# Three accumulation passes per weight tile, each behind its own wait, and a later request for the LayerNorm sums

## The chip, the cores and the metric

The kernel runs on one core of one Trainium2 chip. The metric is device time in microseconds, as the median of three runs. Everything is float32 at the interface; on the chip every large product is made from pairs of reduced-precision parts.

## The reference, cut to what matters

One step of a two-layer streaming encoder, for 512 prompt tokens and 32 decode tokens (544 together), with D_MODEL = 2048:

```python
xp = layer_norm(x_prompt); xs = layer_norm(x_sample)
for l in range(2):
    z = x @ w_in[l]                 # heads of four attention groups, and a gate of 2048 columns
    mk, mv = split(mem_prompt @ w_mem_kv[l])          # 256 memory tokens
    outs = fox(...), band(...), sliding_window(...), cross(..., mk, mv)
    o = concat(outs) * silu(gate)
    x = layer_norm(ALPHA * x + o @ w_out[l])
```

The three products with `w_in`, `w_mem_kv` and `w_out` are nearly all of the work. The outputs are both streams after the second layer, and the keys, values and forget gates of each layer.

## The kernel before, in words

The activations stand transposed in the on-chip memory: 16 chunks of 128 features, each 544 tokens wide, worked on in two halves of 272 tokens. Weights come in tiles of 2048 x 128 (1 MB, `WR`). To keep float32 accuracy every operand is split into a high part and the rest: `WH` (a cast by ScalarE, `w_hi`, line 718) and `WL` = `WR` - `WH` (VectorE, `w_lo`, line 1034) for the weights, `XH` and `XL` for the tokens (`MTH` and `MTL` for the memory tokens). A product is WH*XH + WL*XH + WH*XL, accumulated in one bank of the accumulator memory. Each of the three names `WR`, `WH`, `WL` has two slots, so tile n+2 can be split only when TensorE has finished tile n: ScalarE waits for `zd`, casts and raises `hi`; VectorE waits for `hi`, subtracts and raises `lo`; TensorE waits for `lo`.

There are 184 weight tiles, 92 in each layer, in this order:

- 8 memory tiles (`mem_tile`, line 660), each 48 matmuls of 256 columns: 16 feature chunks k by three products. Between them stand transposes, a small product for the forget gates (`forget`, lines 610 and 617), and in layer 0 the transposes of the input tokens (`turn_x`, lines 639 and 645), which `TURNED` puts at given chunks of tiles 5 to 7.
- 52 head tiles (`gemm_half`, line 424), each two halves of 48 matmuls of 272 columns, with attention work between halves (`scores`, `turn_probs`, `mix`).
- 32 output tiles (`out_tile`, line 441), each 48 matmuls of 272 columns: first 16 tiles for the first half of the tokens (h = 0), then 16 for the second (h = 1). I number the output tiles of a half 0 to 15. Output tile 0 of a half is called with `split`: before each chunk it waits for that chunk of the gated attention output to be split (`ol[hf]`, VectorE's `o_lo`, line 1179; `oh[hf]` is ScalarE's `o_hi`, line 752).

In all three functions the loop over chunks is outside and the three products are inside, so WL is wanted by the second matmul of a tile.

LayerNorm is fused into the output tiles. VectorE adds the residual (line 1438, raises `zf`), subtracts a shift (`centre`, line 1240), adds to a running sum (line 1245), and later adds the squares that ScalarE made (lines 856 and 1250). The shift comes from a small TensorE product with a matrix of ones (`mean_of_first`, line 586, on output tile 0's result; ScalarE's `take_shift`, line 851, passes it on). At the end of a half, TensorE turns the running sums into statistics (`statistics`, line 596), ScalarE's `seed` (lines 862 to 865) and VectorE's `rstd` (lines 1258 to 1263) make the reciprocal deviation, and `normalise` applies it. These TensorE pieces are passed to a tile as `middle`, and run in front of chunk 8 of its 16: the mean in output tile 1 of each half, the sums of h = 0 in output tile 0 of h = 1, and the sums of h = 1 in memory tile 0 of layer 1 (in layer 1 they come after everything).

VectorE executes its instructions in the order written. For output tile c that order is: residual, centre, add up, `w_lo` of tile c+2, squares, `o_lo` or `normalise` or others. So `w_lo` of output tile 2 stands behind `centre` of output tile 0, and so behind the mean. In layer 0, half 0, tile 5 is followed by four subtractions for the next layer's memory tokens (`mem_lo`, line 1236). In layer 0's opening, VectorE's order is written out in `DVE_PLAN`: sums of the input rows, `w_lo` of tiles 2 to 4, the normalisation of the input rows (`first_norm`, line 1321), `w_lo` of tile 5, and then the sample rows (line 1331) and the affine steps, which follow TensorE's transposes.

Of the kernel before, what the change touches and what calls it, by code (L numbers as in the profile page):

```python
# [14 lines left out]
KC = DM // P  # L15
SEQ, DEC, PAST = 512, 32, 256
TOK = SEQ + DEC
HALF = TOK // 2
# [75 lines left out]
NQ = 4  # L94
# [47 lines left out]
def encoder_step(nc, wt, wff, bff, x_t, mem_t, fox_k, fox_v, fox_logf, band_k, band_v, swa_k, swa_v, mem_k, mem_v,  # L142
                 rel_pad, sinks, ln_gt, ln_bt, ident_d, causal_d, swa_mask_d, cos_d, sin_d,
                 y_o, fk_o, fv_o, fl_o, bk_o, bv_o, sk_o, sv_o, mk_o, mv_o):
    with ExitStack() as ctx:
# [6 lines left out]
        def sb(name, shape, dt=F32):  # L152
            size = 4
            for s in shape[1:]:
                size *= s
            off = top[0]
            top[0] += size + -size % 64
            return sb_at(name, shape, off, dt)

        def sem(name):  # L160
            return ctx.enter_context(nc.semaphore(name))

        GB = ctx.enter_context(nc.psum_tensor("GB", [P, 4, 512], F32))
        AB = ctx.enter_context(nc.psum_tensor("AB", [P, 4, 512], F32))

        XH = sb("XH", [P, KC, TOK], F32R)
        XT = sb_at("XT", [P, NT - 1, DM], top[0])
        XL = sb("XL", [P, KC, TOK], F32R)
        OY = sb("OY", [P, KC, TOK])
        WR = sb("WR", [P, 2, KC, P])  # L170
        WH = sb("WH", [P, 2, KC, P], F32R)
        WL = sb("WL", [P, 2, KC, P], F32R)
# [5 lines left out]
        MTH = sb("MTH", [P, KC, NMEM], F32R)  # L178
        MTR = sb_at("MTR", [P, KC, NMEM], top[0])
        MTL = sb("MTL", [P, KC, NMEM], F32R)  # L180
# [78 lines left out]
        hi = sem("hi")  # L259
        lo = sem("lo")  # L260
# [14 lines left out]
        m_hi = sem("m_hi")  # L275
        m_lo = sem("m_lo")
# [46 lines left out]
        oh = [sem("oh0"), sem("oh1")]  # L323
        ol = [sem("ol0"), sem("ol1")]
# [21 lines left out]
        def half(h):  # L346
            return slice(h * HALF, (h + 1) * HALF)
# [68 lines left out]
        def _(pe):  # L416
            def gemm_half(n, s, hf, free):

                if hf == 0:
                    pe.wait_ge(lo, n + 1)  # L420
                    pe.wait_ge(zf[s], free)
                for k in range(KC):
                    for i, (w, x) in enumerate(((WH, XH), (WL, XH), (WH, XL))):
                        mm = pe.matmul(GB[:, 2 * s + hf, 0:HALF], w[:, s, k, :],  # L424
                                       x[:, k, hf * HALF:(hf + 1) * HALF],
                                       start=(k == 0 and i == 0), stop=(k == KC - 1 and i == 2))
                if hf == 1:
                    mm.then_inc(zd, 1)
                return mm

            def out_tile(n, s, hf, free, split=None, middle=None):

                pe.wait_ge(lo, n + 1)
                pe.wait_ge(zf[s], free)
                for k in range(KC):
                    if split is not None:
                        pe.wait_ge(ol[hf], split * KC + k + 1)
                    if k == KC // 2 and middle is not None:
                        middle()
                    for i, (w, x) in enumerate(((WH, XH), (WL, XH), (WH, XL))):  # L440
                        mm = pe.matmul(GB[:, 2 * s + hf, 0:HALF], w[:, s, k, :], x[:, k, half(hf)],  # L441
                                       start=(k == 0 and i == 0), stop=(k == KC - 1 and i == 2))
                mm.then_inc(zd, 1)

            def gemm(n, m, j, hf=None):

                for h in (range(2) if hf is None else [hf]):
                    mm = gemm_half(n + j, j % 2, h, m + j // 2)
                return mm
# [183 lines left out]
            def turn_x(c):  # L633

                if c == 0:
                    pe.wait_ge(s_turn, 16 * N_TURN)
                    pe.wait_ge(x_norm, NT)
                    for k in range(KC):
                        mm = pe.transpose(AB[:, 3, DEC * k:DEC * (k + 1)], XTS[0:DEC, P * k:P * (k + 1)],
                                          ident[0:DEC, 0:DEC])  # L640
                    mm.then_inc(x_turn, 1)
                if c >= 3:
                    pe.wait_ge(nx, c - 2)
                for i in range(NT - 1):
                    mm = pe.transpose(AB[:, c % 3, P * i:P * (i + 1)], XT[:, i, P * c:P * (c + 1)], ident[:, :])
                mm.then_inc(x_turn, 1)

            def mem_tile(l, j, turned, middle=None):
                s, n = j % 2, l * LT + j
                pe.wait_ge(lo, n + 1)  # L650
                pe.wait_ge(zf[s], l * (LT // 2) + j // 2 + 1)
                for k in range(KC):
                    if j == 0 and k % (KC // NQ) == 0:
                        pe.wait_ge(m_lo, NQ * l + k // (KC // NQ) + 1)
                    if k in turned:
                        turn_x(turned[k])
                    if k == KC // 2 and middle is not None:
                        middle()
                    for i, (w, x) in enumerate(((WH, MTH), (WL, MTH), (WH, MTL))):
                        mm = pe.matmul(GB[:, 2 * s, 0:NMEM], w[:, s, k, :], x[:, k, :],  # L660
                                       start=(k == 0 and i == 0), stop=(k == KC - 1 and i == 2))
                mm.then_inc(zd, 1)

            pe.wait_ge(s_one, 1)
            for l in range(DEPTH):
# [7 lines left out]
                for kind, i in PE_PLAN[l]:  # L673
                    if kind == "mem":
                        mem_tile(l, i, TURNED.get(i, {}) if l == 0 else {}, last_sums if l and i == 0 else None)
                    elif kind == "forget":
                        forget(l, range(2) if l == 0 else [i], None if l and i == 0 else last_turn)
                    else:
                        turn_mem(l, i)
# [11 lines left out]
                for h in range(2):  # L691
                    n, m = l * LT + O0 + h * KC, l * (LT // 2) + (O0 + h * KC) // 2 + 1

                    def first_sums():
                        statistics(l + 1, [0])

                    def first_mean():
                        pe.wait_ge(zf[0], m + 1)
                        mean_of_first([half(h)], [h])

                    out_tile(n, 0, h, m, split=l, middle=first_sums if h == 1 else None)
                    out_tile(n + 1, 1, h, m, middle=first_mean)
                    with pe.Fori(1, KC // 2) as q:
                        nc.cur_bb.disable_value_cache()
                        for s in range(2):
                            out_tile(q * 2 + (n + s), s, h, q + m)
# [976 lines left out]
```

## Time and profile before

| | |
|---|---|
| median of 3 runs | 2032.47 us (2031.53 to 2033.11) |
| the profiled execution, its own time | 2032.19 us |
| its span, from the first to the last instruction | 2030.4 us |
| TensorE busy | 1982.9 us, 98% |
| VectorE busy | 1050.4 us, 52% |
| ScalarE busy | 704.8 us, 35% |
| GpSimd busy | 133.2 us, 7% |
| mean granted TensorE clock | 0.995 of full speed |

The profile was taken in one execution. 1.8 us of its time lie outside the span. Times in rows count from the start of the span. A row of the timeline has its start, its duration, the engine, the line, the operation, what it writes and reads, how many instructions are merged in it, and in brackets the idle time in front of it with what ended that. The duration of one matmul includes its latency, so it is longer than the distance to the next one; the rate is read from starts, or from a piece with its count.

### The profile page before, as it was taken

What the parts mean: (1) busy time and instruction counts of PE and PEld (TensorE: products, weight loads), DVE (VectorE), ACT (ScalarE), POOL (GpSimd) and SP (SyncE); (2) the same over time, 40 slices, a digit from 0 to 9 for tenths busy, and PEclk for the clock granted to TensorE, in tenths of its full rate; (3) what the DMA queues carried; (4) which work ended last, traced back from release to release, by engine and by line L of the source; (5) the groups of instructions that cost most, each with busy time, mean ns of one, the idle gap of its engine ahead of it and who ended that gap; (6) DMA issues with size and microseconds to landing.
All of it is one profiled execution on the core that took longest, in us unless ns stands there. A gap on an engine that the chain in (4) does not pass through costs nothing.

```text
span 2030.4 us, 38182 instructions
## 1 busy us (share of the span) xinstructions
PE 1982.9 (98%) x15868; PEld 1958.2 (96%) x15868; DVE 1050.4 (52%) x1649; ACT 704.8 (35%) x1053; POOL 133.2 (7%) x238
## 2 busy tenths in 40 slices
PE   6999999999999999999999999999999999999995
PEld 6999999999999999999999999999999999999995
DVE  6743343333465445777884334334335545566777
ACT  6432232222233233544563232222222322344444
POOL 0110000000000000000001001000000000000000
PEclk9999999999999999999999999999999999999998
DMA  7632232222222222555664223232222222225463
GB/s 303 222 139 96 105 106 80 104 96 92 93 72 97 71 88 90 194 193 185 225 210 150 89 105 107 78 105 85 92 104 89 79 75 82 102 90 193 185 213 136
DMA packets 55051, 254.75 MB, mean 125 GB/s; under 512 B 9469, under 2 KB 19325, under 8 KB 30865
## 3 DMA queue, kind: packets, MB, share of 16 engines
q1 hardware_dynamic: 31184, 202.68, 27.9%
q0 software_dynamic: 13344, 36.51, 5.2%
q10 hardware_dynamic: 10432, 14.29, 1.9%
q8 instruction: 65, 1.06, 0.2%
q14 instruction: 26, 0.21, 0.0%
HBM read 228.36 MB, written 27.70 MB: 126 GB/s over the span
## 4 chain that ended last, share of the span: by engine, by line
PE 94%; DVE 3%; DMA 1%; ACT 1%; issue 1%; SPq 0%; ACTq 0%; DVEq 0%
PE GB L424 62%; PE GB L441 18%; PE AB L470 3%; PE AB L513 3%; PE GB L660 3%; PE AB L481 2%; DMA WR<-in_wt 1%; DVE WL L1034 1%; PE AB L610 1%; ACT WH L718 1%; PE AB L518 0%; PE AB L498 0%; PE AB L521 0%; PE AB L617 0%; DVE OY L1275 0%
## 5 line engine op out<-in xcount | busy, mean ns | idle before, releaser
L424 PE MATMUL GB<-XH,WH 128*128 128x272 f32 x3328 | 965.0, 290 | 0.0
L424 PE MATMUL GB<-XL,WH 128*128 128x272 f32 x3328 | 958.4, 288 | 0.0
L424 PE MATMUL GB<-XH,WL 128*128 128x272 f32 x3328 | 957.9, 288 | 0.0
L424 PEld LDWEIGHTS GB<-XH,WH 128*128 128x128 f32 x3328 | 626.4, 188 | 1.5
L424 PEld LDWEIGHTS GB<-XH,WL 128*128 128x128 f32 x3328 | 626.4, 188 | 0.0
L424 PEld LDWEIGHTS GB<-XL,WH 128*128 128x128 f32 x3328 | 625.3, 188 | 0.0
L718 ACT CAST WH<-WR 128x2048 fp32r<-128x2048 f32 x184 | 351.2, 1909 | 746.6 <-PE GB L424 531.6
L1034 DVE TENSOR_TENSOR WL<-WR,WH 128x2048 fp32r<-128x2048 f32 x184 | 421.3, 2290 | 342.2 <-ACT WH L718 341.9
L441 PE MATMUL GB<-XH,WH 128*128 128x272 f32 x1024 | 296.2, 289 | 4.1 <-DVE WL L1034 4.1
L441 PE MATMUL GB<-XL,WH 128*128 128x272 f32 x1024 | 296.3, 289 | 0.0
L441 PE MATMUL GB<-XH,WL 128*128 128x272 f32 x1024 | 294.1, 287 | 0.0
L441 PEld LDWEIGHTS GB<-XH,WH 128*128 128x128 f32 x1024 | 192.6, 188 | 5.5 <-issue 5.2
L441 PEld LDWEIGHTS GB<-XH,WL 128*128 128x128 f32 x1024 | 192.9, 188 | 0.2
L441 PEld LDWEIGHTS GB<-XL,WH 128*128 128x128 f32 x1024 | 192.4, 188 | 0.0
L731 ACT ACTIVATE S<-S,nmx 128x256 f32<-128x256 f32 (+8 forms) x160 | 83.8, 524 | 175.3 <-DVE nmx L1076 173.6
L660 PE MATMUL GB<-MTH,WH 128*128 128x256 f32 x256 | 76.4, 298 | 19.1 <-DVE MTL L1236 11.7
L1141 DVE SCALAR_TENSOR_TENSOR SPL<-GB,SPL 128x544 fp32r<-128x544 f32 x24 | 17.3, 720 | 141.1 <-ACT SPL L777 141.1
L1107 DVE SCALAR_TENSOR_TENSOR GA<-ES,GB 128x544 f32<-128x544 f32 x30 | 21.5, 718 | 119.2 <-ACT ES L746 119.2
L1093 DVE COPY PT<-AB 128x512 f32<-128x512 f32 x64 | 40.1, 669 | 71.5 <-PE AB L481 71.5
L660 PE MATMUL GB<-MTL,WH 128*128 128x256 f32 x256 | 73.8, 288 | 0.0
L660 PE MATMUL GB<-MTH,WL 128*128 128x256 f32 x256 | 73.7, 288 | 0.0
L1076 DVE TENSOR_REDUCE nmx<-S 128x1 f32<-128x256 f32 (+8 forms) x160 | 69.8, 436 | 5.5
(178 smaller groups left out, 1640.9 us busy)
## 6 DMA issues: line engine op xcount, KB each, us to landing
WR<-in_wt SPq DMA_DIRECT2D x184, 1024.0 KB, 4.8
XR<-out POOLq DMA_DIRECT2D x64, 136.0 KB, 2.8
out<-OY ACTq DMA_DIRECT2D x24, 272.0 KB, 2.2
out<-OY ACTq DMA_DIRECT2D x8, 544.0 KB, 5.7
out<-KT POOLq DMA_DIRECT2D x16, 272.0 KB, 2.5
out<-VT POOLq DMA_DIRECT2D x16, 272.0 KB, 2.3
XT<-in_x_t SPq DMA_DIRECT2D x4, 1024.0 KB, 13.5
BI<-nc_rows POOLq DMA_DIRECT2D x8, 400.0 KB, 4.0
```

The lines of the kernel that those rows point to most:

```text
L424: mm = pe.matmul(GB[:, 2 * s + hf, 0:HALF], w[:, s, k, :], x[:, k, hf * HALF:(hf + 1) * HALF], start=(k == 0 and i == 0), stop=(k == KC - ...
L441: mm = pe.matmul(GB[:, 2 * s + hf, 0:HALF], w[:, s, k, :], x[:, k, half(hf)], start=(k == 0 and i == 0), stop=(k == KC - 1 and i == 2))
L470: mm = pe.matmul(AB[0:r, b, at:at + w], q[:, t0:t0 + r], k, start=(p == 0), stop=(p == 2))
L481: mm = pe.transpose(AB[:, j // 4, P * (j % 4):P * (j % 4 + 1)], S[:, at:at + P], ident[:, :])
L513: mm = pe.matmul(AB[:, 3, P * i:P * (i + 1)], V[:, kb, :], pt_col(j), start=(b == 0), stop=(b == len(g.blocks[i]) - 1))
L660: mm = pe.matmul(GB[:, 2 * s, 0:NMEM], w[:, s, k, :], x[:, k, :], start=(k == 0 and i == 0), stop=(k == KC - 1 and i == 2))
L718: act.copy(WH[:, s, :, :], WR[:, s, :, :]).then_inc(hi, 1)
L731: act.activation(s, s, ACT.Exp, bias=nmx[0:r, i:i + 1], accum_out=esum[0:r, i:i + 1]).then_inc(ex, 1)
L1034: dve.tensor_tensor(WL[:, s, :, :], WR[:, s, :, :], WH[:, s, :, :].bitcast(F32), ALU.subtract).then_inc(lo, 1)
L1076: dve.tensor_reduce(nmx[0:r, i:i + 1], S[0:r, at:at + w + g.sink], AX_X, ALU.max, negate=True).then_inc(mk, 1)
L1093: dve.tensor_copy(PT[:, 512 * b:512 * b + w], AB[:, b, 0:w]).then_inc(pte, 1)
L1107: dve.scalar_tensor_tensor(split2(GA[:, :]), split2(ES[:, :]), 1.0, z2(s), ALU.add, ALU.mult) \
```

## The change

In `gemm_half`, `out_tile` and `mem_tile` the nesting is turned round: the 48 matmuls of a half are now 16 of WH*XH, then 16 of WL*XH, then 16 of WH*XL. The tile begins behind `hi`, and `lo` is waited for only in front of the second pass. In a `split` tile the first pass waits for `oh` chunk by chunk and the third for `ol`; there chunk 15 is kept for the end of the tile in all three products. The same order of `out_tile` is used for all output tiles. `mem_tile` waits for the split memory tokens in the same way (`m_hi`, then `m_lo`). `middle` runs in front of matmul 40 of 48 in `out_tile`, where it ran in front of matmul 24; in `mem_tile` it stays at 24, and the transposes of `TURNED` stay at the same matmul numbers. Everything else is the same, and so are the number and the shapes of all instructions that compute.

```diff
             def gemm_half(n, s, hf, free):
                 if hf == 0:
-                    pe.wait_ge(lo, n + 1)
+                    pe.wait_ge(hi, n + 1)
                     pe.wait_ge(zf[s], free)
-                for k in range(KC):
-                    for i, (w, x) in enumerate(((WH, XH), (WL, XH), (WH, XL))):
+                for i, (w, x) in enumerate(((WH, XH), (WL, XH), (WH, XL))):
+                    if hf == 0 and i == 1:
+                        pe.wait_ge(lo, n + 1)
+                    for k in range(KC):
                         mm = pe.matmul(GB[:, 2 * s + hf, 0:HALF], w[:, s, k, :],
...
             def out_tile(n, s, hf, free, split=None, middle=None):
-                pe.wait_ge(lo, n + 1)
+                pe.wait_ge(hi, n + 1)
                 pe.wait_ge(zf[s], free)
-                for k in range(KC):
+                early = range(KC - 1)
+                order = [(i, k) for i in range(3) for k in early] + [(i, KC - 1) for i in range(3)]
+                for at, (i, k) in enumerate(order):
+                    w, x = ((WH, XH), (WL, XH), (WH, XL))[i]
+                    if at == KC - 1:
+                        pe.wait_ge(lo, n + 1)
                     if split is not None:
-                        pe.wait_ge(ol[hf], split * KC + k + 1)
-                    if k == KC // 2 and middle is not None:
+                        if i == 0:
+                            pe.wait_ge(oh[hf], split * KC + k + 1)
+                        if i == 2:
+                            pe.wait_ge(ol[hf], split * KC + k + 1)
+                    if at == 5 * KC // 2 and middle is not None:
                         middle()
...
             def mem_tile(l, j, turned, middle=None):
                 s, n = j % 2, l * LT + j
-                pe.wait_ge(lo, n + 1)
+                pe.wait_ge(hi, n + 1)
                 pe.wait_ge(zf[s], l * (LT // 2) + j // 2 + 1)
-                for k in range(KC):
-                    if j == 0 and k % (KC // NQ) == 0:
-                        pe.wait_ge(m_lo, NQ * l + k // (KC // NQ) + 1)
-                    if k in turned:
-                        turn_x(turned[k])
-                    if k == KC // 2 and middle is not None:
-                        middle()
-                    for i, (w, x) in enumerate(((WH, MTH), (WL, MTH), (WH, MTL))):
+                for i, (w, x) in enumerate(((WH, MTH), (WL, MTH), (WH, MTL))):
+                    if i == 1:
+                        pe.wait_ge(lo, n + 1)
+                    for k in range(KC):
+                        at = i * KC + k
+                        if j == 0 and k % (KC // NQ) == 0 and i != 1:
+                            pe.wait_ge(m_lo if i else m_hi, NQ * l + k // (KC // NQ) + 1)
+                        if at % 3 == 0 and at // 3 in turned:
+                            turn_x(turned[at // 3])
+                        if at == 3 * KC // 2 and middle is not None:
+                            middle()
```

## Rows read from the trace of the kernel before

**Rows 1.** The profile's page, busy time of each engine with its share and instructions.
```profile
PE 1982.9 (98%) x15868; PEld 1958.2 (96%) x15868; DVE 1050.4 (52%) x1649; ACT 704.8 (35%) x1053; POOL 133.2 (7%) x238
```
**Rows 2.** TensorE's waits: whom it waited for, us in total, times, longest.
```profile
PE GB L660 <- DVE MTL L1236: 11.7, 1, 11.7
PE GB L660 <- DVE WL L1034: 7.4, 5, 2.1
PE AB L596 <- DVE LNB L1250: 5.6, 3, 2.0
PE GB L441 <- DVE WL L1034: 4.1, 5, 1.0
```
**Rows 3.** Timeline of VectorE, the opening.
```profile
41.56 2.28 DVE L1034 TENSOR_TENSOR WL<-WR,WH 128x2048 fp32r<-128x2048 f32 x1
47.53 1.33 DVE L1321 TENSOR_SCALAR XTS<-XTS,XST 32x2048 f32<-32x2048 f32 x1
48.79 2.27 DVE L1034 TENSOR_TENSOR WL<-WR,WH 128x2048 fp32r<-128x2048 f32 x1
53.24 0.69 DVE L1331 TENSOR_TENSOR OY<-AB,gT 128x512 f32<-128x512 f32 x1 [2.18 <-PE AB L639]
```
**Rows 4.** Timeline of TensorE, the opening.
```profile
28.50 0.39 PE L660 MATMUL GB<-MTH,WH 128*128 128x256 f32 x1 [1.87 <-DVE WL L1034]
36.58 0.38 PE L660 MATMUL GB<-MTH,WH 128*128 128x256 f32 x1 [2.12 <-DVE WL L1034]
52.02 1.18 PE L639 MATMUL AB<-ident,XTS 32*128 32x32 f32 x16
```
**Rows 5.** Stretches of the opening: busy time by engine, clock, DMA share, GB/s.
```profile
29.00:34.00 5.00, 5.00 (x45) 5.00 (x44) 4.12 (x4) 2.06 (x3) 0.00 (x0) 1.00 1.04 397
36.50:40.00 3.50, 3.42 (x18) 3.42 (x19) 0.47 (x4) 3.23 (x7) 0.00 (x0) 0.61 0.61 204
```
**Rows 6.** Timeline around the first mean: TensorE and VectorE.
```profile
827.93 0.62 PE L586 MATMUL AB<-OY,ones 128*128 128x272 f32 x2
...
829.91 2.29 DVE L1034 TENSOR_TENSOR WL<-WR,WH 128x2048 fp32r<-128x2048 f32 x1
...
832.33 0.39 PE L441 MATMUL GB<-XH,WH 128*128 128x272 f32 x1 [0.77 <-DVE WL L1034]
832.56 0.29 PE L441 MATMUL GB<-XH,WL 128*128 128x272 f32 x1
832.68 0.28 PE L441 MATMUL GB<-XL,WH 128*128 128x272 f32 x1
```
**Rows 7.** Timeline at output tile 8 of the first half, TensorE.
```profile
868.62 0.29 PE L441 MATMUL GB<-XL,WH 128*128 128x272 f32 x1
869.95 0.39 PE L441 MATMUL GB<-XH,WH 128*128 128x272 f32 x1 [1.05 <-DVE WL L1034]
```
**Rows 8.** Timeline at the sums of the first half, layer 0, TensorE.
```profile
921.37 0.29 PE L441 MATMUL GB<-XL,WH 128*128 128x272 f32 x1
923.41 1.15 PE L596 MATMUL AB<-LNB,ones 128*128 128x272 f32 x4 [1.76 <-DVE LNB L1250]
```
**Rows 9.** Timeline at memory tile 2 of layer 1, TensorE.
```profile
1031.22 0.28 PE L660 MATMUL GB<-MTL,WH 128*128 128x256 f32 x1
1032.96 0.39 PE L660 MATMUL GB<-MTH,WH 128*128 128x256 f32 x1 [1.45 <-DVE WL L1034]
```
**Rows 10.** Pieces of the chain that ended last: start, us, what, matmuls.
```profile
89.48 30.13 PE GB L424 x240
819.05 9.04 PE GB L441 x72
869.95 48.70 PE GB L441 x384
934.81 84.40 PE GB L441 x672
1044.85 17.08 PE GB L660 x144
```

More of the change, by code:

```diff
@@ L431, in out_tile @@
             def out_tile(n, s, hf, free, split=None, middle=None):
-                pe.wait_ge(lo, n + 1)
+                pe.wait_ge(hi, n + 1)
                 pe.wait_ge(zf[s], free)
-                for k in range(KC):
-                    if split is not None:
-                        pe.wait_ge(ol[hf], split * KC + k + 1)
-                    if k == KC // 2 and middle is not None:
+                early = range(KC - 1)
[4 more added lines that the diff above has]
+                        pe.wait_ge(lo, n + 1)
+                    if split is not None:
+                        if i == 0:
[3 more added lines that the diff above has]
+                    if at == 5 * KC // 2 and middle is not None:
                         middle()
-                    for i, (w, x) in enumerate(((WH, XH), (WL, XH), (WH, XL))):
-                        mm = pe.matmul(GB[:, 2 * s + hf, 0:HALF], w[:, s, k, :], x[:, k, half(hf)],
-                                       start=(k == 0 and i == 0), stop=(k == KC - 1 and i == 2))
+                    mm = pe.matmul(GB[:, 2 * s + hf, 0:HALF], w[:, s, k, :], x[:, k, half(hf)],
+                                   start=(at == 0), stop=(at == 3 * KC - 1))
                 mm.then_inc(zd, 1)
@@ L649, in mem_tile @@
                 s, n = j % 2, l * LT + j
-                pe.wait_ge(lo, n + 1)
+                pe.wait_ge(hi, n + 1)
                 pe.wait_ge(zf[s], l * (LT // 2) + j // 2 + 1)
-                for k in range(KC):
-                    if j == 0 and k % (KC // NQ) == 0:
-                        pe.wait_ge(m_lo, NQ * l + k // (KC // NQ) + 1)
-                    if k in turned:
-                        turn_x(turned[k])
-                    if k == KC // 2 and middle is not None:
-                        middle()
-                    for i, (w, x) in enumerate(((WH, MTH), (WL, MTH), (WH, MTL))):
+                for i, (w, x) in enumerate(((WH, MTH), (WL, MTH), (WH, MTL))):
[9 more added lines that the diff above has]
+                            middle()
                         mm = pe.matmul(GB[:, 2 * s, 0:NMEM], w[:, s, k, :], x[:, k, :],
-                                       start=(k == 0 and i == 0), stop=(k == KC - 1 and i == 2))
+                                       start=(at == 0), stop=(at == 3 * KC - 1))
                 mm.then_inc(zd, 1)
```

## The prediction

> **What bounds the kernel now.** I read the page first: TensorE is busy 98% of the span and VectorE 52% [rows 1], so time can come only from TensorE's idle time or from the pace of its matmuls. The view of TensorE's waits then gives the idle time: 11.7 us before its first matmul, five waits for WL in the memory tiles, 7.4 us, three for the running sums, 5.6 us, and five for WL in the output tiles, 4.1 us [rows 2]. Nothing else holds it. I then went to the timeline at each wait, to see who is late and what that engine was held by. The pace comes from the chain: 240 head matmuls in 30.13 us, 672 of the output tiles in 84.40 us, 125.5 ns each; 144 memory matmuls in 17.08 us, 118.6 ns each [rows 10]. One pass of 16 is therefore 2.0 us (1.9 in a memory tile). That is what the change gives each tile: the deadline for `lo` moves 2.0 us back, and the tile begins behind `hi`, which is ready at least one VectorE subtraction (2.29 us, [rows 6]) earlier. A tile that now waits less than 2.0 us for WL loses its wait; one that waits longer, or whose WL moves back too, does not.
>
> **The opening (gain 3.0 us).** Here WL is not late because of TensorE but because of VectorE's and ScalarE's own queues, so gains of successive tiles do not add up: each tile ends at its `lo` plus two passes, where it ended at `lo` plus three. Memory tile 4: VectorE ends its WL at 41.56 + 2.28 = 43.84 [rows 3]. Two passes later (32 x 118.6 ns = 3.8) TensorE is at 47.6. Memory tile 5 now starts on its WH pass and comes after six matmuls (0.7 us) to the transposes of the input rows, at 48.4. These need the last normalised rows, which VectorE has at 47.53 + 1.33 = 48.86 [rows 3]. So they start at about 49.0, where they start at 52.02 [rows 4]: 3.0 us. WL of tile 5 (48.79 + 2.27 = 51.06 [rows 3]) is asked for ten matmuls and one more set of transposes later, past 52, and no longer holds anything. Next in line is VectorE: it waited 2.18 us for those transposes before the sample rows at 53.24 [rows 3], and can start them at 51.1, 2.1 us earlier; the remaining 0.9 us of TensorE's lead meet VectorE's short waits for later transposes, so I keep 3.0 and take 2.1 as the low end. The first matmul itself comes earlier too (it waits only for MTH, not MTL), but memory tiles 1 to 4 wait for weights that have their own pace, so nothing is added for it. The upper end is 4.0: tile 5's own pass and the transposes in it.
>
> The clock: an idle time of 1.87 us in front of 28.50 left it at 2.4 GHz (granted 1.00 in the stretch behind it), one of 2.12 us in front of 36.58 was followed by a stretch with 0.61, mostly at the 1.2 GHz level [rows 4, 5]. After the change idle times there are 2.0 us or less, so it may stay up. I count nothing for it: tile 4 then waits for its own WH anyway.
>
> **Output tiles, the mean (gain 0).** The wait of 0.77 us in output tile 2 stands 4.40 us behind the mean: 827.93 to 832.33 [rows 6]. Between them lie ScalarE's shift, `centre`, the sum and `w_lo`, all behind the mean. Now the mean runs 16 matmuls later and `lo` is wanted 16 matmuls later. Both move together: 24 matmuls lie between them before and after (8 + 16 in place of 24). Four such waits, two in each layer, make up 4 x 0.77 = 3.1 of the 4.1 us that the output tiles wait for WL [rows 2]; they stay, inside the tile between the WH*XH and the WL*XH pass. The two moves together cost nothing and bring nothing here.
>
> **Output tile 8, layer 0, first half (gain 1.3 us).** WL is late behind `mem_lo`, which hangs on tile 5. The distance of starts is 869.95 - 868.62 = 1.33 us for a normal 0.13, and the restart costs 0.1 (832.33 to 832.56 is 0.23 us, the next distance 0.12 [rows 6]). 1.33 < 2.0, so it all goes: 1.2 + 0.1 = 1.3 [rows 7]. Layer 1 has no such wait.
>
> **The sums (gain 1.9 us in each layer).** The sums start at 923.41, 2.04 us after the last matmul at 921.37 [rows 8]. They are held by VectorE's squares of the half before. Asked for 16 matmuls later (2.0 us), they start at the same moment, but the 16 matmuls are already done. 2.04 - 0.13 = 1.9; the three waits of the view include the layer 1 one, of the same length, and the last after all tiles, which the change does not touch. What follows (ScalarE's seed, `rstd`, then the residual and the mean) starts at the same moment as before and is wanted at the same moment, because the mean too has moved 16 matmuls back. So 3.8 for both.
>
> **Memory tile 2, layer 1 (gain 1.7 us).** WL stands behind `rstd`, which hangs on sums at matmul 24 of tile 0, unchanged. The distance of starts is 1.73 us [rows 9] for 0.12; with the restart 1.7, less than the 1.9 of a pass. What is late next is the split of the last tokens for the forget gates (line 617); VectorE makes it right behind, and TensorE asks for it after a whole tile, 5.7 us.
>
> **The waits themselves (0).** There are 184 new waits for `lo`, and in the four split tiles 16 more each. The piece of 240 head matmuls holds two tile borders with two met waits each and runs at 125.5 ns throughout; the piece of 72 from 819.05 holds output tile 0 with its 16 met waits for `ol` and takes 9.04 us, 125.6 ns each [rows 10]. So a met wait costs nothing that I can see; the other bound is a restart of 0.1 us each [rows 6]. I take 0, the value of the rows that show the thing itself. Queued behind the new wait is the rest of the tile, and behind that everything; ScalarE's next `w_hi` waits for the tile's end, as before.
>
> A rule of the Trainium skill speaks against this. Its page Perfetto Trace Analysis, section Identifying Dependency Chains, says that waits beyond an instruction's own can become separate instructions in front of it, and the page Advanced Engine Details and Errata, section Network/Comms, gives 50 to 100 ns for reading a semaphore from the sequencer; by that 184 waits would be an estimated 9 to 18 us. By that rule the time would be no better or worse than now. The trace does not show the price at any met wait, as said.
>
> **The order of the matmuls (0).** Their number, shapes and bank are the same. Which weight part is loaded while which token part streams is the same set of pairs, only k differs. But the pace is not one number: the 384 matmuls from 869.95 take 48.70 us; without the restart and the tail of the last one (some 0.3) that is 126.1 ns, where the 672 later ones have 125.2 to 125.6 [rows 10]. I can't tell what sets this. The bounds for the new order are 125.0 and 126.1, that is -0.5 and +0.6 ns on 13,056 matmuls of 272 columns (104 head tiles of 96, 64 output tiles of 48): -6.5 to +8 us. I take 0.
>
> **The sum.** 3.0 + 1.3 + 3.8 + 1.7 = 9.8 us. 2032.2 - 9.8 = 2022.4 for the profiled execution; the median of the runs is 0.3 above it: 2022.7.
>
> **The rivals.**
> - A, the pace moves. For it: 125.2 and 126.1 ns stand in the same loop. Against: the piece over three kinds of pairs is even. A slow pace gives 2022.7 + 8 = 2030.7, a fast one 2016.2.
> - B, slower than before: each new wait breaks the run of weight loads and costs a restart, 184 x 0.1 = 18.4 us, so 2041. It decides from 9.8/184 = 53 ns a wait; the time is then above 2032.5. For it: a wait that holds costs 0.1 us. Against it: the pieces with met waits.
> - C, given back: TensorE's lead in the opening and in layer 1's memory tiles is lost again to VectorE and to the transfers, as VectorE is little idle there. Only the sums and tile 8 stay: 3.8 + 1.3 = 5.1, so 2027.4.
> - D, the moved mean is not neutral: if the chain behind it reaches later tiles (output tile 3, or the residuals that free the bank), each of four places costs up to a pass of 2.0, 8 us, and leaves 2030.7.
>
> **Chances.** Forecast (2018.5 to 2026) 0.58; A slow 0.12, A fast 0.08; B 0.07; C 0.10; D 0.05. The range 2016 to 2030 takes in the forecast, C, and all of both A but the slow end, and leaves out B and D. A measurement of this kernel can tell 0.2%, 4 us, from no change. Faster by more than that, below 2028.4: the forecast, A fast, C and a third of A slow, 0.80. Within: the rest of A slow and D, 0.13. Slower: B, 0.07.
>
> **What would show it.** In TensorE's waits of the changed kernel: the sums wait once (2 us, at the end) instead of three times; four waits of about 0.8 us are left in the output tiles, now between WH*XH and WL*XH matmuls, none at tile 8; layer 1's memory tile 2 starts without idle time; the first matmul starts earlier than 11.7 and the transposes of the sample rows near 49. The step on the waits is wrong if borders between passes show more than 0.13 us. The step on the pace is wrong if 48 matmuls of an output tile take more than 6.07 or less than 5.98 us. The prediction is wrong if TensorE's busy pieces are longer by some 10 us in sum, or if new waits stand where there were none.

## The result and the profile after

The changed kernel takes 2021.13 us (median of 4, 2020.73 to 2021.17) where the one before takes 2032.79 (median of 4): a ratio of 0.9944, 95% interval 0.9931 to 0.9956. The forecast was 2022.7, with a range of 2016 to 2030. The profiled execution took 2021.17 us, its span 2019.4 us against 2030.4 before.

The page of the kernel after, span and busy times:

```profile
span 2019.4 us, 38302 instructions
PE 1981.5 (98%) x15868; PEld 1956.7 (97%) x15868; DVE 1049.7 (52%) x1649; ACT 705.0 (35%) x1053; POOL 133.4 (7%) x238
```

TensorE is busy for 1.4 us less than in [rows 1], and the span is 11.0 us shorter: what went is idle time and, it turns out, a little pace. The view of TensorE's waits, with its total, times and the longest, to set against [rows 2]. Lines have moved: L450 is `out_tile`, L672 `mem_tile`, L1046 `w_lo`, L605 the sums, L859 the cast of the memory tokens, L907 the copy of a memory tile out of its bank.

```profile
PE GB L672 <- ACT MTH L859: 8.9, 1, 8.9
PE GB L450 <- DVE WL L1046: 3.3, 4, 0.8
PE GB L672 <- ACT MT L907: 2.4, 2, 2.1
PE AB L605 <- DVE LNB L1262: 2.0, 1, 2.0
PE GB L672 <- DVE WL L1046: 1.6, 2, 1.4
PE GB L672 <- ACT WH L730: 0.6, 1, 0.6
PE AB L648 <- DVE XTS L1333: 0.3, 1, 0.3
```

The sums wait once instead of three times. Four waits for WL of 0.8 us are left in the output tiles, one fewer than before. In the memory tiles five waits for WL have become two, and waits for WH and for the bank have come up in their place.

The timeline of TensorE after, with rows left out at each `...`: the opening's transposes; the mean in output tile 1 (line 595) and the wait behind it in tile 2; the first pass of output tile 8; the sums and the matmuls behind them; and the start of layer 1's memory tile 2. At the edge of a stretch a row has only the matmuls inside the stretch.

```profile
48.98 1.15 PE L648 MATMUL AB<-ident,XTS 32*128 32x32 f32 x16 [0.34 <-DVE XTS L1333]
...
826.57 0.62 PE L595 MATMUL AB<-OY,ones 128*128 128x272 f32 x2
...
828.77 1.27 PE L450 MATMUL GB<-XH,WH 128*128 128x272 f32 x9
830.88 0.64 PE L450 MATMUL GB<-XH,WL 128*128 128x272 f32 x3 [0.84 <-DVE WL L1046]
...
865.12 1.17 PE L450 MATMUL GB<-XH,WH 128*128 128x272 f32 x8
...
918.17 1.08 PE L605 MATMUL AB<-LNB,ones 128*128 128x272 f32 x4
918.88 0.99 PE L450 MATMUL GB<-XL,WH 128*128 128x272 f32 x5
...
1024.50 0.76 PE L672 MATMUL GB<-MTH,WH 128*128 128x256 f32 x5
```

A row without brackets had no idle time in front of it that the view counts. The transposes start at 48.98 where [rows 4] has 52.02. Output tile 8, the sums and layer 1's memory tile 2 (1024.50) have lost the waits of [rows 7, 8, 9]. The wait behind the mean is still 0.84 us, where [rows 6] has 0.77, but it now stands between WH*XH and WL*XH.

How far TensorE's tiles are ahead of the kernel before gives the account. The lead is the difference of the starts of the same tile in the two timelines, taken before rounding, and the last column is how much it changed since the row above. The rows without a layer are layer 0's:

| up to the start of | before, us | after, us | lead | this step |
|---|---|---|---|---|
| layer 0, memory tile 6 | 60.93 | 57.85 | 3.07 | opening 3.07 |
| output tile 0 | 818.89 | 815.58 | 3.31 | 52 head tiles 0.24 |
| output tile 7 | 862.69 | 859.12 | 3.58 | 0.27 |
| output tile 8 | 869.95 | 865.12 | 4.84 | 1.26 |
| second half, tile 0 | 918.48 | 913.12 | 5.37 | 0.53 |
| second half, tile 1 | 927.40 | 920.08 | 7.32 | sums 1.96 |
| second half, tile 3 | 940.92 | 933.73 | 7.19 | -0.13 |
| layer 1, memory tile 1 | 1025.64 | 1018.80 | 6.84 | -0.35 |
| layer 1, memory tile 2 | 1032.96 | 1024.50 | 8.46 | 1.62 |
| layer 1, output tile 0 | 1809.55 | 1800.73 | 8.82 | 0.36 |
| layer 1, second half, tile 0 | 1907.83 | 1898.27 | 9.56 | 0.74 |
| layer 1, second half, tile 1 | 1916.75 | 1905.24 | 11.52 | sums 1.96 |
| end | 2030.39 | 2019.37 | 11.02 | -0.50 |

### The profile page after: what moved, and what is told of

Same layout as the page of the kernel before. It is cut to its first block, busy times and chain, and to the rows that moved or that the text cites. A ratio compares the mean times of both kernels' runs of the same rounds, so it can differ in the third digit from the quotient of the medians.

```text
span 2019.4 us, 38302 instructions
## 1 busy us (share of the span) xinstructions
PE 1981.5 (98%) x15868; PEld 1956.7 (97%) x15868; DVE 1049.7 (52%) x1649; ACT 705.0 (35%) x1053; POOL 133.4 (7%) x238
## 4 chain that ended last, share of the span: by engine, by line
PE 96%; DVE 2%; DMA 1%; ACT 1%; issue 0%; SPq 0%; ACTq 0%; DVEq 0%
PE GB L426 62%; PE GB L450 19%; PE AB L479 3%; PE AB L522 3%; PE GB L672 3%; PE AB L490 2%; DMA WR<-in_wt 1%; PE AB L619 1%; DVE WL L1046 1%; PE AB L527 0%; PE AB L507 0%; PE AB L530 0%; PE AB L626 0%; PE AB L654 0%; PE AB L494 0%; DVE OY L1287 0%
## 5 line engine op out<-in xcount | busy, mean ns | idle before, releaser
L1046 DVE TENSOR_TENSOR WL<-WR,WH 128x2048 fp32r<-128x2048 f32 x184 | 421.4, 2290 | 344.3 <-ACT WH L730 344.0
L426 PE MATMUL GB<-XH,WH 128*128 128x272 f32 x3328 | 458.1, 290 | 0.0
L426 PE MATMUL GB<-XL,WH 128*128 128x272 f32 x3328 | 451.3, 287 | 0.0
L426 PE MATMUL GB<-XH,WL 128*128 128x272 f32 x3328 | 451.2, 287 | 0.0
L426 PEld LDWEIGHTS GB<-XL,WH 128*128 128x128 f32 x3328 | 431.2, 189 | 0.0
L426 PEld LDWEIGHTS GB<-XH,WL 128*128 128x128 f32 x3328 | 431.2, 189 | 0.0
L426 PEld LDWEIGHTS GB<-XH,WH 128*128 128x128 f32 x3328 | 429.5, 188 | 1.5
L450 PE MATMUL GB<-XH,WL 128*128 128x272 f32 x1024 | 149.7, 288 | 3.3 <-DVE WL L1046 3.3
L450 PE MATMUL GB<-XL,WH 128*128 128x272 f32 x1024 | 151.3, 288 | 0.0
L450 PE MATMUL GB<-XH,WH 128*128 128x272 f32 x1024 | 149.2, 287 | 0.0
L450 PEld LDWEIGHTS GB<-XH,WL 128*128 128x128 f32 x1024 | 136.4, 188 | 4.2 <-DVE WL L1046 4.2
L450 PEld LDWEIGHTS GB<-XL,WH 128*128 128x128 f32 x1024 | 137.1, 188 | 0.5
L450 PEld LDWEIGHTS GB<-XH,WH 128*128 128x128 f32 x1024 | 136.3, 188 | 0.0
L479 PE MATMUL AB<-SPL 128*128 128x256 f32 (+6 forms) x552 | 70.3, 279 | 0.0
L479 PEld LDWEIGHTS AB<-SPL 128*128 128x128 f32 (+1 forms) x552 | 64.7, 164 | 4.1
L522 PE MATMUL AB<-PT,V 128*128 128x128 f32 x560 | 67.6, 275 | 0.0
```

The lines of the kernel that those rows point to most:

```text
L479: mm = pe.matmul(AB[0:r, b, at:at + w], q[:, t0:t0 + r], k, start=(p == 0), stop=(p == 2))
L522: mm = pe.matmul(AB[:, 3, P * i:P * (i + 1)], V[:, kb, :], pt_col(j), start=(b == 0), stop=(b == len(g.blocks[i]) - 1))
L1046: dve.tensor_tensor(WL[:, s, :, :], WR[:, s, :, :], WH[:, s, :, :].bitcast(F32), ALU.subtract).then_inc(lo, 1)
```

## The experiments

Each time stands against the kernel before, run beside it on the same chip; the edits shown are against the changed kernel, but for the second one, which is against the kernel before. Its median there was 2033.1 in the first group (passes alone, deeper alone, the first order alone, memory tiles as before), 2033.8 in the second, 2033.3 for the last run. The changed kernel's own runs were not repeated beside them, so a difference from 2021.1 is good to about a microsecond: the median of the kernel before moved by that much between the groups and the result above (2032.8 to 2033.8).

**The passes without the later mean and sums.**

```diff
-                    if at == 5 * KC // 2 and middle is not None:
+                    if at == 3 * KC // 2 and middle is not None:
```

> The changed kernel with the mean and the sums back in front of matmul 24 of their output tiles; the three passes and their waits stay. My theory: the two halves of the change touch different waits. With the mean at 24 and lo wanted at matmul 15 of output tile 2, 39 matmuls (4.9 us) lie between them against a chain of 4.4 us, so the four waits of 0.8 us behind the mean (in all 3.7 us with restarts) vanish, while the two waits for the sums of 1.9 us each come back: +3.8 - 3.7, so about 2021.2 us, as the changed kernel. In the trace: TensorE waits for LNB three times, for WL in the output tiles not at all. Rival: the later place of the mean is what the kernel gains by, and the mean's waits stay wherever it is; then both come back and the time is about 2025.

Measured: 2020.76 us, ratio 0.9941 (0.9927 to 0.9954). TensorE's waits:

```profile
PE AB L605 <- DVE LNB L1262: 5.5, 3, 2.0
PE GB L672 <- ACT MT L907: 3.2, 3, 1.7
```

Three waits for the sums are back and none for WL is left in the output tiles. By the starts of the tiles against the changed kernel, each mean gives 1.09 us (four of them, 4.4) and each set of sums takes 1.99 (two, 4.0). So the second half of the change, as it was made, is worth nothing in sum: what the sums gain the mean gives back.

**The later mean and sums without the passes.** Both stand 15 matmuls later than in the kernel before (16 in the change), in the old order of matmuls.

```diff
-                    if k == KC // 2 and middle is not None:
+                    if k == 13 and middle is not None:
```

> The kernel before with its own order of matmuls and waits, and only the mean and the sums moved, from matmul 24 to matmul 39 of their output tiles (chunk 13). My theory: the two waits for the sums shrink by 15 matmuls (1.9 us each, -3.7 us in all), and each of the four waits behind the mean grows by the same 1.9 us, as lo is still wanted at the tile's start (+7.5 us): slower by 3.8 us, about 2036.6 us, with waits for WL of 2.6 us in output tile 2. Rival: the move is good by itself and gives 2029.

Measured: 2039.65 us, ratio 1.0031 (1.0021 to 1.0042), slower, and 3 us more than I expected. The steps I had named are there: every mean costs 1.88 us more and every set of sums 1.88 less. What I had not counted is the clock. TensorE's timeline and two stretches of it, behind the last mean (busy times by engine, granted clock, DMA share, GB/s):

```profile
1930.78 0.59 PE L441 MATMUL GB<-XH,WH 128*128 128x272 f32 x1 [2.66 <-DVE WL L1034]
...
1932.00:1937.00 5.00, 5.00 (x24) 5.00 (x23) 4.22 (x5) 0.29 (x1) 0.19 (x1) 0.50 0.77 280
1937.00:1940.00 3.00, 3.00 (x26) 3.00 (x25) 0.14 (x1) 0.14 (x1) 0.00 (x0) 1.00 0.63 262
```

Behind an idle time of 2.66 us the granted clock is 0.50, its 1.2 GHz level: 24 matmuls take 5 us where 26 take 3. That place lost 2.8 us more than the longer wait explains. Of the four waits of this length two came with such a fall, and the other fall cost 1.3 us; a third fall, in the opening, cost 1.5 us. With these three, 5.5 us, and the expected 3.8 the profiled execution is at 2041.6 us; the median of the runs is 2 us lower.

**The order of matmuls alone.** `lo` at the tile's start, mean and sums at matmul 24, and the low parts of the tokens (`ol`, `m_lo`) waited for in the first pass.

```diff
-                        if i == 0:
-                            pe.wait_ge(oh[hf], split * KC + k + 1)
-                        if i == 2:
-                            pe.wait_ge(ol[hf], split * KC + k + 1)
...
+                    if split is not None and i == 0:
+                        pe.wait_ge(ol[hf], split * KC + k + 1)
```

> The changed order of matmuls (three passes), with everything else as in the kernel before: the tile waits for lo at its start, split tiles and memory tile 0 wait for the low parts in the first pass, the mean and the sums stand at matmul 24. It isolates the pace of the new order. The two traces already show the changed kernel's lead over the one before growing by 0.05 us a tile in the first half of the output tiles and shrinking by 0.025 in the second, and 1.2 us in sum over both layers. Theory: that is the order's own pace, so 2032.8 - 1.2 = 2031.6, with every idle time of the kernel before still there. Rival (pace and waits hang together): exactly 2032.8, and the lead per tile is not there.

Measured: 2037.46 us, ratio 1.0024 (1.0015 to 1.0033), slower than both my theory and its rival. It changed more than the order of matmuls, and what it did is instructive. TensorE's and VectorE's timelines at output tile 0 of the second half:

```profile
919.75 1.94 PE L443 MATMUL GB<-XH,WH 128*128 128x272 f32 x14
924.94 0.60 PE L443 MATMUL GB<-XH,WH 128*128 128x272 f32 x1 [3.25 <-DVE XL L1182]
...
924.45 0.79 DVE L1182 TENSOR_TENSOR XL<-OY,XH 128x272 fp32r<-128x272 f32 x2
```

With passes, chunk 14 is wanted at the 15th matmul of the tile and not at the 43rd, but its low part is split only behind a `w_lo` on VectorE, which ends at about 924.2. So each pass must wait for its own operand; that is what the separate waits of the change are for, beyond WL. With the idle time the clock fell too (granted 0.51 in the stretch behind it).

**The same with the waits for `oh`, `ol`, `m_hi` and `m_lo` as in the change.** Only `lo` at the tile's start and the place of mean and sums differ from the changed kernel.

```diff
-                pe.wait_ge(hi, n + 1)
+                pe.wait_ge(lo, n + 1)
...
-                    if at == KC - 1:
-                        pe.wait_ge(lo, n + 1)
...
-                    if at == 5 * KC // 2 and middle is not None:
+                    if at == 3 * KC // 2 and middle is not None:
```

> The three passes as in the changed kernel, with their waits for oh, ol, m_hi and m_lo, but lo is waited for at the tile's start and the mean and the sums stand at matmul 24. The first run of the order alone had also put the wait for ol into the first pass, which held TensorE for up to 3.3 us twice and let its clock fall. Theory: without that the order is worth its pace, 1.2 us over both layers, and every idle time of the kernel before is there: 2033.1 - 1.2 = 2031.9. Rival: the order by itself is slow in some other way, 2035 or more.

Measured: 2030.99 us, ratio 0.9990 (0.9981 to 0.9999), against 2031.9 expected. Its median is 2.8 us below that of the kernel before in its group, where the pace gives 1.2 us; but the interval reaches from 0.2 to 3.9 us below, so that the rest isn't clear of noise. Five waits for WL in the output tiles, 4.2 us, and three for the sums, 5.5 us, stand as in the kernel before. The pieces of its chain, to be read against [rows 10]:

```profile
869.36 48.28 PE GB L446 x384
...
933.81 84.75 PE GB L446 x672
```

The same 384 matmuls take 48.28 us where the old order took 48.70, and the same 672 take 84.75 where it took 84.40. So the order changes the pace by -1.1 ns a matmul in the first half of the tokens and +0.5 ns in the second, with no wait in sight.

**Memory tiles as before, all else changed.** `mem_tile` is the old function.

> The changed kernel with the 16 memory tiles put back as they were (product by product inside a chunk, lo at the tile's start); head and output tiles stay changed. Theory: the opening loses 3.1 us and memory tile 2 of layer 1 another 1.7, so 2021.1 + 4.8 = 2025.9. Rival: the opening's lead was bounded by VectorE and is made up later anyway, then only the 1.7 us come back, 2022.8.

Measured: 2026.25 us, ratio 0.9966 (0.9954 to 0.9978). Against the changed kernel its memory tile 6 of layer 0 starts 3.1 us later (60.97 against 57.85), and memory tile 2 of layer 1 loses another 1.62. That is my theory, and the rival (2022.8) falls.

**The price of a met wait.** A wait for `hi`, long raised, in front of every fourth matmul of head and output tiles.

```diff
+                        if k % 4 == 2:
+                            pe.wait_ge(hi, n + 1)
                         mm = pe.matmul(GB[:, 2 * s + hf, 0:HALF], w[:, s, k, :],
```

> The changed kernel with a wait for hi, long met, in front of every fourth matmul of head and output tiles: 3,264 waits more. It prices a met wait. Theory: nothing, 2021.1 within 2 us, no distance between starts of 0.2 us in front of them. Rival: a restart of 0.1 us each, 326 us; at 53 ns each, the point from which 184 new waits would have cost the change's gain, 173 us.

Measured: 2021.36 us (2020.50 to 2022.35), ratio 0.9937 (0.9924 to 0.9951). The piece of the chain behind the first mean of layer 0, in this kernel (L454) and then in the changed one (L450):

```profile
830.62 87.44 PE GB L454 x697
```

```profile
830.88 87.45 PE GB L450 x697
```

The same 697 matmuls, with the added waits among them, take the same time to 0.01 us. By the medians the 3,264 waits cost 0.2 us in all, less than the spread of the runs.

What kind of wait this prices is in the trace's records of TensorE's instructions. In the changed kernel 749 weight loads carry a wait of their own, in this one 3,983, which is 3,234 more; the other 30 added waits are semaphore instructions of their own, 190 in place of 160. (The page counts 40540 instructions where the changed kernel has 38302; the other 2,208 are register instructions.) So the run shows that a met wait which rides on a weight load is free; it hardly tests a met wait that is an instruction of its own. The change is of the first kind too: from the kernel before to the changed one the weight loads with a wait go from 492 to 749, and the semaphore instructions stay 160.

**Mean at matmul 24, sums at 40.**

```diff
-            def out_tile(n, s, hf, free, split=None, middle=None):
+            def out_tile(n, s, hf, free, split=None, middle=None, place=40):
...
-                    if at == 5 * KC // 2 and middle is not None:
+                    if at == place and middle is not None:
...
-                    out_tile(n + 1, 1, h, m, middle=first_mean)
+                    out_tile(n + 1, 1, h, m, middle=first_mean, place=24)
```

> The changed kernel with the mean back in front of matmul 24 of output tile 1, and the sums left in front of matmul 40 of output tile 0. If the two halves of the change touch different waits, as the run with the passes alone says, both sets go: the four waits for WL of 0.8 us (3.7 us with restarts) leave the changed kernel and the sums' waits stay away. In the second half the mean can come at most 0.5 us after its place, as rstd and the residual end 5.3 us after the sums start. So 2021.1 - 3.7 + up to 1.0: 2017.4 to 2018.4 us. Rival: mean and sums are coupled through the order of VectorE, and with the sums late and the mean early TensorE waits for the residual for 1 us or more in each layer; then 2019.5 or more.

Measured: 2017.50 us (2017.24 to 2017.83), ratio 0.9918 (0.9905 to 0.9932). All four waits for WL behind the mean are gone and the sums wait only at the end. In the second half the mean makes TensorE lose 0.4 us. Two rows of TensorE and, between them, one of VectorE:

```profile
920.84 1.29 PE L450 MATMUL GB<-XH,WL 128*128 128x272 f32 x9
921.77 0.43 DVE L1450 SCALAR_TENSOR_TENSOR OY<-XR,GB 128x272 f32<-128x272 f32 x1
922.25 0.73 PE L595 MATMUL AB<-OY,ones 128*128 128x272 f32 x2
```

Nine matmuls from 920.84 end their slot at 921.97 at 125.5 ns each, and the mean starts at 922.25, just behind the residual (line 1450), which VectorE ends at 922.20. The residual stands behind `rstd` on VectorE, as expected.

**Low weights last.** The passes are WH*XH, WH*XL, WL*XH, so that `lo` is wanted at matmul 30 or 32. Split tiles and memory tile 0 keep their order.

```diff
-                for i, (w, x) in enumerate(((WH, XH), (WL, XH), (WH, XL))):
-                    if hf == 0 and i == 1:
+                for i, (w, x) in enumerate(((WH, XH), (WH, XL), (WL, XH))):
+                    if hf == 0 and i == 2:
...
```

> The changed kernel with its passes in the order WH*XH, WH*XL, WL*XH (in split tiles and memory tile 0 of a layer they stay as they are), so that lo is wanted at matmul 30 or 32 and not at 15 or 16. Theory (a WL wait is paid only by what it exceeds the passes in front of it): the mean's four waits of 0.8 us, which the change left, go as well, 2021.1 - 3.7 = 2017.4; the opening stays as it is, since it hangs on the normalised rows. Rival (the waits follow the matmuls that can run before them, as VectorE falls behind further): the waits move on into the third pass and nothing is gained, 2021.1.

Measured: 2016.94 us (2016.56 to 2017.91), ratio 0.9917 (0.9904 to 0.9931), the lowest of all by median. No wait for WL is left in the view of TensorE's waits. Behind the first mean, output tile 2 runs through its three passes without a break:

```profile
828.17 2.01 PE L450 MATMUL GB<-XH,WH 128*128 128x272 f32 x15
830.02 2.05 PE L450 MATMUL GB<-XL,WH 128*128 128x272 f32 x15
831.91 2.04 PE L450 MATMUL GB<-XH,WL 128*128 128x272 f32 x15
```

**Both together.**

> Low weights last and the mean at matmul 24, together. Each alone brought 3.6 to 4.3 us by the trace. If both take away the same four waits behind the mean, the two together bring no more than the better one: 2016.5 to 2017.9, with no wait for WL in the output tiles, and 0.4 us in front of the second half's mean. If they act on different things, they add: 2013.

Measured: 2017.86 us (2017.57 to 2018.33), ratio 0.9925 (0.9911 to 0.9939). They don't add: both take away the same four waits, and the early mean brings its own 0.4 us in each layer. The three versions lie within 1 us of each other, which these runs don't put in an order; each is 3.3 to 4.2 us faster than the changed kernel.

## Why the prediction was right, point by point

- **Opening, 3.0 us.** 3.07 by the lead at memory tile 6. The transposes start at 48.98, predicted 49.0, with the normalised rows as the releaser. What I had left out is the tile's second wait at its start, for the bank: in [rows 4] it was hidden behind `lo`. Memory tile 3 now waits for ScalarE's copy of tile 1 and not for its own WH:

```profile
34.07 0.36 ACT L907 COPY MT<-GB 128x256 f32<-128x256 f32 x1
...
34.58 0.98 PE L672 MATMUL GB<-MTH,WH 128*128 128x256 f32 x3 [2.09 <-ACT MT L907]
```

  So I had the idle time there as at most 2.0 us, and it was 2.09, and the clock fell with it (granted 1.00 from 33.0 to 34.4, 0.50 from 34.5 to 37.8), as it had in [rows 5] after 2.12. It cost nothing, because memory tile 4 waits for its bank anyway. The run with the mean at 24 shows it: there the same idle time is 2.08 us, the clock stays at 1.00, TensorE then waits 1.19 us for the bank of tile 4, and that tile starts at 41.80 where it starts at 41.84 with the fall. That it would not matter was in the prediction; that the clock "may stay up" did not come true in this execution.
- **The mean, 0.** From the start of output tile 1 to that of tile 3 the lead changes by 0.01 to 0.02 us in the two first halves and by -0.13 to -0.14 in the two second ones; without the pace (below) about -0.1 us at each place. The wait moved inside the tile with its length. The prediction counted one matmul too many: `out_tile` asks for `lo` in front of matmul 15 and not 16, so 8 + 15 = 23 matmuls lie between mean and wait, and one matmul is 0.125 us. `w_lo` behind the mean starts 1.4 us earlier on the clock than in [rows 6] (828.54 against 829.91) with a lead of 3.3 to 3.4 us: relative to the tiles it is 2.0 us later, as worked out. The runs add what the prediction did not ask: this near zero is a loss of 1.1 us a place against leaving the mean where it was.
- **Output tile 8, 1.3 us.** 1.26 in the step, of which 0.05 is pace, and the restart's 0.1 in the step behind it. Right.
- **The sums, 1.9 us each.** 1.96 us in each layer. Right.
- **Memory tile 2 of layer 1, 1.7 us.** 1.62 at its start and 0.1 within it. Right.
- **The waits, 0.** Settled by the run with 3,264 of them, for waits that ride on a weight load, as the added ones of the change do. Rival B falls: at its 0.1 us each that run would have been 326 us slower, and it was slower by 0.2. The page of the Trainium skill that I had set against the trace (Advanced Engine Details and Errata, section Network/Comms) gives 50 to 100 ns for reading a semaphore from the sequencer; an estimate from its lower figure is 163 us. The trace doesn't agree: a stream of matmuls did not pay that for a met wait here.
- **The pace, 0.** This term was mis-sized, within its bounds. The lead grows by 0.05 us a tile in the first half of the output tiles, shrinks by 0.025 in the second and grows by 0.2 to 0.25 over 52 head tiles: about 1.2 us in all. Both order runs show it, with the waits left in place. That is the difference between 9.8 and the 11.0 of the spans; the 0.1 us lost at each mean and the 0.3 us that the other terms brought above their sizes nearly cancel.
- **What is left.** The medians differ by 11.7 us and the profiled executions by 11.0. In its groups of 4 to 19 runs the kernel before spreads over 1.7 to 4.7 us, and the changed one, in four runs, over 0.4. My reading is that the clock falls at different places from one execution to another (at 37.2 us in the profile before; at 28.9 and 52.8 in the run with the deeper mean, whose opening is the same code; its memory tile 6 starts 1.7 us later, 1.5 of it behind the second fall), and the changed opening has slack where the old one had none. That is shown for single executions, not for the medians. Transfers move it too: in the run of the passes alone, whose opening is the changed one, ScalarE gets the weights of memory tile 3 at 31.75 and not at 32.27, and everything up to the output tiles is 0.5 us earlier.
- **Rivals.** C (given back, 2027.4) falls: no wait came back in the heads or in layer 1's memory tiles. D falls: output tile 3 and later ones have no wait. Of A, the pace moved the fast way, but by less than a fifth of its bound (1.2 of 6.5 us).

## What to carry to other kernels

A wait is worth the shorter of two things: its own length, and the work that can be put in front of it. For each wait, write down what it hangs on: if that is earlier work of the same engine a fixed number of instructions back, what counts is the distance between the two. Here the mean and the wait behind it were moved together and gained nothing. To widen the distance at one end gained 3.6 us (the mean back to matmul 24) or 4.2 (the low weights in the last pass); to narrow it, with the mean alone moved later, cost 1.9 us at each of the four places and more where the clock fell. When a loop nest is turned so that operands are used in passes, every other operand's deadline moves too, and needs a wait at its own pass.

## What the runs showed of the hardware that I had not expected

- A met wait that rides on a weight load costs TensorE's stream nothing measurable: 3,264 added waits, of which 3,234 are of this kind, cost 0.2 us in all.
- The pace of a matmul of 272 columns depends on the order alone, by about 1 ns of 125: the same 384 matmuls took 48.70 us interleaved and 48.28 us in passes, and in the other half of the tokens it went the other way, 84.40 and 84.75 for 672. No run here shows why.
- The length of the last idle time alone doesn't tell whether TensorE's clock falls. It fell with idle times of 2.09 and 2.12 us and stayed up with one of 2.08; it stayed up with 1.87 us in the kernel before (28.50) and fell with 1.87 us at the same place in the second run of the order alone (granted 0.50 from 30.1 to 33.4). With four of about 2.65 us it fell twice. A fall cost 1.3 to 2.8 us on top of the wait where TensorE was the bound, and nothing where the next tile waited for its bank. What decides it no run here shows.
